# Conv feed-forward: the order of ScalarE's chunk split and first tap, and the place of a pair's activation split

## The reference, cut to what matters

```python
def causal_dwconv(u, w, b):
    C = u.shape[-1]
    y = lax.conv_general_dilated(u, w[:, None, :].astype(u.dtype), window_strides=(1,),
                                 padding=[(CONV_W - 1, 0)],
                                 dimension_numbers=('NWC', 'WIO', 'NWC'),
                                 feature_group_count=C)
    return y + b
...
def first_block(x, attn_norm, w_in, nsa_q_norm, nsa_k_norm, cmp_pos_k, cmp_pos_v, cmp_w1_k, cmp_w2_k,
              cmp_w1_v, cmp_w2_v, gla_w_gate2, gla_b_gate, gla_out_norm, w_out, ffn_norm, w_up,
              conv_w, conv_b, w_down):
...
        h = h + jnp.concatenate([o_nsa, o_gla], axis=-1) @ w_out[l]
        u = causal_dwconv(rms_norm(h, ffn_norm[l]) @ w_up[l], conv_w[l], conv_b[l])
        gate, up = jnp.split(u, 2, axis=-1)
        h = h + (jax.nn.silu(gate) * up) @ w_down[l]
    return h
...
def swiglu(hn, w_ffn_in, w_ffn_out):
    gate, up = jnp.split(hn @ w_ffn_in, 2, axis=-1)
    return (jax.nn.silu(gate) * up) @ w_ffn_out
```

## Time and profile before

| | us |
|---|---|
| median of 3 runs | 2320.32 |
| lowest, highest | 2319.63, 2327.05 |
| span of the profiled execution | 2316.6 |
| TensorE matmuls busy | 2205.7 |
| TensorE weight loads busy | 1700.6 |
| VectorE busy | 1116.4 |
| ScalarE busy | 806.4 |
| GpSimd busy | 67.8 |

### The profile page before, as it was taken

One profiled execution on the slowest core, in us unless ns is written; L12 is line 12 of the kernel. 1 busy time (PEld: TensorE's weight loads), 2 busy tenths in 40 slices (PEclk: granted clock), 3 DMA queues, 4 the chain that ended last, 5 costly groups with the idle time before them and its releaser, 6 DMA issues. The chain is left out here.

```text
span 2316.6 us, 32721 instructions
## 1 busy us (share of the span) xinstructions
PE 2205.7 (95%) x13572; PEld 1700.6 (73%) x13572; DVE 1116.4 (48%) x1800; ACT 806.4 (35%) x1310; POOL 67.8 (3%) x88
## 2 busy tenths in 40 slices
PE   8999799999999999989998999998999999999999
PEld 7776457777778898976765788766566578888887
DVE  3464675666653367654334534436332244444422
ACT  3332554333332443332224222225346533223221
POOL 0000001000000000000000000000012102000000
PEclk8999899999999999999999999999999999999999
DMA  4224001222232244331224321214721232322322
GB/s 161 65 72 154 1 1 64 82 91 82 87 105 92 78 145 130 124 110 59 66 69 146 130 92 62 70 55 150 247 69 55 91 115 91 95 96 91 98 94 91
DMA packets 78595, 218.65 MB, mean 94 GB/s; under 512 B 8688, under 2 KB 13168, under 8 KB 78448
## 3 DMA queue, kind: packets, MB, share of 16 engines
q1 hardware_dynamic: 78448, 216.57, 28.2%
HBM read 185.74 MB, written 29.75 MB: 93 GB/s over the span
## 5 line engine op out<-in xcount | busy, mean ns | idle before, releaser
L296 PE MATMUL ps<-nx_hi,whi 128*128 128x264 f32 (+1 forms) x1504 | 539.1, 358 | 17.0 <-DVE nx_lo L385 9.6
L281 DVE TENSOR_TENSOR wlo<-raw,whi 128x1024 fp32r<-128x1024 f32 x282 | 346.3, 1228 | 400.4 <-ACT whi L274 400.0
L298 PE MATMUL ps<-nx_hi,wlo 128*128 128x264 f32 (+1 forms) x1504 | 512.9, 341 | 0.0
L297 PE MATMUL ps<-nx_lo,whi 128*128 128x264 f32 (+1 forms) x1504 | 512.8, 341 | 0.0
L274 ACT ACTIVATE whi<-raw 128x1024 fp32r<-128x1024 f32 x282 | 297.8, 1056 | 520.9 <-PE ps L298 416.5
L296 PEld LDWEIGHTS ps<-nx_hi,whi 128*128 128x128 f32 x1504 | 287.0, 191 | 84.6 <-issue 45.3
L298 PEld LDWEIGHTS ps<-nx_hi,wlo 128*128 128x128 f32 x1504 | 287.1, 191 | 32.6
L297 PEld LDWEIGHTS ps<-nx_lo,whi 128*128 128x128 f32 x1504 | 287.7, 191 | 30.4 <-issue 1.9
L296 PE MATMUL ps<-x_hi,whi 128*128 128x512 f32 x528 | 209.8, 397 | 14.9 <-DVE wlo L281 14.9
L298 PE MATMUL ps<-x_hi,wlo 128*128 128x512 f32 x528 | 209.8, 397 | 0.0
L297 PE MATMUL ps<-x_lo,whi 128*128 128x512 f32 x528 | 208.4, 395 | 0.0
(11 more groups left out here) (460 smaller groups left out, 2869.9 us busy)
## 6 DMA issues: line engine op xcount, KB each, us to landing
raw<-stream_dram SPq DMA_DIRECT2D x285, 512.0 KB, 3.5
qk_spill<-ring SPq DMA_DIRECT2D x16, 264.0 KB, 2.2
qk_cols<-qk_spill SPq DMA_DIRECT2D x16, 264.0 KB, 4.0
v_spill<-ring SPq DMA_DIRECT2D x16, 264.0 KB, 2.1
v_cols<-v_spill SPq DMA_DIRECT2D x16, 264.0 KB, 4.3
dz_spill<-ring SPq DMA_DIRECT2D x16, 256.0 KB, 2.1
dz<-dz_spill SPq DMA_DIRECT2D x16, 256.0 KB, 5.1
sbk_spill<-ring SPq DMA_DIRECT2D x8, 264.0 KB, 2.1
```

The source lines that it names most:

```text
L281: dve.tensor_tensor(K.wlo[:, n % HL], K.raw[:, n % RAW], K.whi[:, n % HL].bitcast(F32), ALU.subtract).then_inc(K.s_lo, 1)
L296: pe.matmul(out, whi, xhi, start=start, stop=False, skip_group_check=skip)
L297: pe.matmul(out, whi, xlo, start=False, stop=False, skip_group_check=skip)
L298: return pe.matmul(out, wlo, xhi, start=False, stop=stop, skip_group_check=skip)
```

## The change

Only the case `conv` is altered; with `conv` false the order stays what it was. On ScalarE `hi_of` of the gate's chunk is issued before the gate's first tap, and `hi_of` of the up chunk before the up half's first tap. The high part of a pair's activation is issued behind the first tap of the next pair's gate, its low part on VectorE behind the other taps of the next pair's gate. The last pair's stays at its end. No instruction is added or taken out.

```diff
--- before.py
+++ after.py
@@ -521,21 +521,26 @@
                     scaled_hi(act, K.h[:, d], gain_ffn[:, d:d + 1], x_tile(d)[0]).then_inc(z["x_hi"], 1)
                     square("squares", "summed", d, d + 1)
                 factor_root(K, act, z)
+
+                def full_hi(p):
+                    act.wait_ge(z["act_full"], p + 1)
+                    act.activation(act_tile(p)[0], up[:, p % 2], ACT.Copy).then_inc(z["act_hi"], 1)
                 for p in range(FT):
                     pb, s = p % 2, up0 + 2 * p
                     ps = [K.ps[:, (KT + 2 * p + kind) % 4, :] for kind in range(2)]
                     if p >= 2:
                         act.wait_ge(z["act_lo"], p - 1)
-                    if p == 0:
+                    if p == 0 or conv:
                         hi_of(act, s, s, 0)
                     act.wait_ge(z["scaled"], 2 * p + 1 if conv else p + 1)
                     if conv:
                         act.activation(g[:, pb], ps[0], ACT.Identity, scale=w1[:, 0, p:p + 1, 2],
                                        bias=b1[:, 0, p:p + 1]).then_inc(z["first_tap"], 1)
                         if p > 0:
-                            hi_of(act, s, s, 0)
+                            full_hi(p - 1)
                         act.wait_ge(z["convolved"], 2 * p + 1)
                         act.activation(g[:, pb], g[:, pb], ACT.Silu).then_inc(z["silu"], 1)
+                        hi_of(act, s + 1, s + 1, 0)
                         act.wait_ge(z["scaled"], 2 * p + 2)
                         act.activation(up[:, pb], ps[1], ACT.Identity, scale=w1[:, 1, p:p + 1, 2],
                                        bias=b1[:, 1, p:p + 1]).then_inc(z["first_tap"], 1)
@@ -543,9 +548,9 @@
                         act.activation(g[:, pb], ps[0], ACT.Silu).then_inc(z["silu"], 1)
                         if p > 0:
                             hi_of(act, s, s, 0)
-                    hi_of(act, s + 1, s + 1, 0)
-                    act.wait_ge(z["act_full"], p + 1)
-                    act.activation(act_tile(p)[0], up[:, pb], ACT.Copy).then_inc(z["act_hi"], 1)
+                        hi_of(act, s + 1, s + 1, 0)
+                    if not conv or p == FT - 1:
+                        full_hi(p)
                 for _, kind, i in ends:
                     if kind == 0:
                         hi_of(act, down0 + i, down0 + i, 0)
@@ -586,6 +591,11 @@
                 lo_of(dve, up0, up0, 0)
                 factor_made(K, dve, z, rs[:])
                 dve.wait_ge(z["factor_made"], 1)
+
+                def full_lo(p):
+                    dve.wait_ge(z["act_hi"], p + 1)
+                    ah, al = act_tile(p)
+                    dve.tensor_tensor(al, up[:, p % 2], ah.bitcast(F32), ALU.subtract).then_inc(z["act_lo"], 1)
                 for p in range(FT):
                     pb, s = p % 2, up0 + 2 * p
                     for kind in range(2):
@@ -602,6 +612,8 @@
                                     y[:, 1:SEQ], ps[:, 0:SEQ - 1], w1[:, kind, p:p + 1, 1], y[:, 1:SEQ], ALU.mult, ALU.add))
                                 dve.scalar_tensor_tensor(y[:, 2:SEQ], ps[:, 0:SEQ - 2], w1[:, kind, p:p + 1, 0], y[:, 2:SEQ],
                                                          ALU.mult, ALU.add).then_inc(z["convolved"], 1)
+                                if kind == 0 and p > 0:
+                                    full_lo(p - 1)
                             elif p > 0:
                                 lo_of(dve, s + kind, s + kind, 0)
                         else:
@@ -615,9 +627,8 @@
                         dve.wait_ge(z["convolved"], 2 * p + 2)
                         dve.wait_ge(z["silu"], p + 1)
                         dve.tensor_tensor(up[:, pb], up[:, pb], g[:, pb], ALU.mult).then_inc(z["act_full"], 1)
-                    dve.wait_ge(z["act_hi"], p + 1)
-                    ah, al = act_tile(p)
-                    dve.tensor_tensor(al, up[:, pb], ah.bitcast(F32), ALU.subtract).then_inc(z["act_lo"], 1)
+                    if not conv or p == FT - 1:
+                        full_lo(p)
                 for _, kind, i in ends:
                     if kind == 0:
                         lo_of(dve, down0 + i, down0 + i, 0)
```

## The result

The changed kernel takes 2303.49 us as the median of five executions (2297.21 to 2304.18), the kernel before 2321.63 beside it (2319.63 to 2327.05). The ratio on record is 0.9903, with a 95% interval of 0.9889 to 0.9918; it is not the quotient of the two medians, which is 0.9922. By either the change is about one per cent faster. The profiled execution took 2297.21 us, its span is 2295.4 (before 2316.6); in every execution on record the time lies 1.8 us above the span. Both kernels scatter by some 7 to 11 us from one execution to the next. So sizes are read from starts and spans, and verdicts from ratios.

What follows compares the result with a forecast made beforehand. A ScalarE-VectorE ping-pong of 12.32 us a pair was taken to bound the first block's feed-forward. 227.80 - 37 x 5.60 = 20.6 us less gives span 2296.0, forecast 2299.7 us, range 2295 to 2306.

Steps and rivals of the forecast that it cites:

- From span to time: Whole kernel: the page's span lies 3.7 us under the median; the same distance turns span 2296.0 into 2299.7 us.
- What bounds: First block's feed-forward: ScalarE and VectorE wait for each other in turn, 12.32 us a pair, making TensorE start late.
- The loop: VectorE's time per pair in the up-projection when it never waits for TensorE: from 12.32 down to 8.40 us.
- The residue before the up chunk's low part: VectorE's wait for the up chunk's high part: about 0.42 us of the 1.79 stays.
- Part (a) alone is enough: Gate chunk's split ahead of the gate's first tap: alone leaves VectorE's loop at 10.47 us, already under 11.20.
- What is late next: After VectorE is level, no TensorE stall left in the stretch; last activation's low part ready some 6 us after last unit.
- The unit: One weight chunk's 24 matmuls on TensorE, taken as 5.60 us; 37 units then give 20.6 us less.
- rival 2: Second block's waits of TensorE give back gain, up to 4.3 us either way, 2296 to 2304; chance 0.12.
- Bounds: ScalarE and VectorE working at once: no cost taken; at most 24% more VectorE work, a loop of 10.3 us.
- Rival 1: VectorE's loop still binds, over 11.20 us, needing 36% more work; at 45% the time is 2312; chance 0.04.
- Rival 3: Change does nothing because transfers make TensorE late: pair stays at 12.32 us, time 2320; chance 0.04.
- Rival 4: Splits waiting for late transfers hold up ScalarE's taps; decides from landing 8.8 us, at 11 gives 2344; chance 0.03.

Runs made afterwards that it cites:

- the other session: The changed kernel run again unaltered beside the follow-up kernels: 2303.0 us over six executions, ratio 0.9919 to the kernel before.
- part (c): Only the activation's split deferred behind the next gate's taps, both weight splits left behind the first taps, against the kernel before: 2307.33 us, ratio 0.9938.
- Part (a) alone: Only the gate chunk's split put ahead of the gate's first tap, on the kernel before: 2304.84 us, ratio 0.9917.
- the first two runs with late transfers: Up-projection load of chunk n also waits until unit n-2 is used: changed kernel 2329.43 us, ratio 1.0013; kernel before 2341.97, ratio 1.0070.

## Why the prediction was right

The forecast was 2299.7 us, in a range of 2295 to 2306; measured were 2303.49 and in the other session 2303.0. The mechanism and the gain of the stretch are right. The step from span to median is not, and that the median fell into the range all the same is in part luck (see *From span to time*).

- *What bounds*: right. The ping-pong set the pace, and each part that shortens it alone makes the kernel faster.
- *The loop*: forecast 8.40 us, measured 8.22, with a backlog and with the five added products taken off again. The difference is in sizes. An instruction of VectorE that waits for nothing begins before the one ahead has ended: the scaling at 407.42 is 0.69 us long, and the low part behind it begins after 0.60, at 408.02. So a wait that goes saves its length and 0.09 us more. The same makes part (c) 0.79 us, a pair of 11.53 instead of 11.68. The residue before the up chunk's low part was put at 0.42 and is 0.44, by two terms that cancel: VectorE's two instructions after the taps were put at 1.38 us and take 1.20 (410.68 to 411.88), ScalarE's at 1.80 and take 1.65 (to 412.33). VectorE is level with TensorE in the third pair; three or four were forecast.
- *Part (a) alone is enough*: right; 10.47 was forecast, and 11.17 less its wait is 10.4 to 10.5.
- *What is late next*: right. The last activation's low part was put at 6 us after the last unit, far ahead of its use; it ends at 639.21, 6.1 us after that unit's end at 633.13, and no wait of TensorE is left.
- *The unit*: 5.60 us was taken from the second block, 5.59 is what this stretch has (11.17 a pair). The forecast of 20.6 us was 0.5 low: the stretch gave 21.1. The span was forecast at 2296.0 and is 2295.4.
- *Everything behind moves up whole* (rival 2): at 761.04 it still does. At the end the spans differ by 21.2, so next to nothing was given back in the profiled executions.
- *From span to time*: this step was wrong. The 3.7 us between the page's span and the median were taken as fixed. In every execution on record the time lies 1.8 us above its span, so 1.9 of the 3.7 were scatter. The profiled execution took 2297.21 us, 2.5 under the forecast: these 1.9, and 0.6 in the span. The median is 3.8 above the forecast, since three of the five executions took 2303 to 2304 us, and so outside the 1.5 us to which I gave a chance of 0.77. No term of the sum and no part of the range stood for the scatter of 7 us from one execution to the next; the range was wide enough because of the 4.3 us of rival 2, which the profiled executions don't show. By medians of the same session the gain is 18.1 us (2321.63 - 2303.49) and 19.3 (2322.25 - 2303.0).
- *Bounds*: ScalarE and VectorE at work together cost nothing that can be read: the low part still takes 1.23 us, the scaling 0.70.
- *Rival 1* needed 36% more work on VectorE. Three added products, 2.1 us or 26% of 7.87, were free and five, 45%, were not. *Rival 3* fell with part (a): the pair went to 11.17 us with the transfers as they were. *Rival 4* stays untested. Its 8.8 us count from a load's issue to its landing, while my late transfers land, by the sum 5.6 + 3.4, some 9 us after the end of the unit from which their split could otherwise start, and 3.4 after their issue. My expectation for the first of these runs took the one for the other. They show that a late transfer reaches TensorE in the new order sooner than in the old, by a chain that the prediction hadn't worked out.

## What to carry to other kernels

When two engines wait for each other in turn, write the loop as a sum of work and waits for one of them and hold it against the pace of the engine that ought to bound; the gain here was the difference, and no more, however many waits are removed. On an engine that takes its queue in order, put first what waits only for things that are ready long before, and behind it what waits for the partner engine: one line moved in this way (the gate chunk's split ahead of the first tap) gave the whole gain, 20.5 us by spans. What is hidden then has a margin, here about 3 us of VectorE's work a pair, that can be measured by adding idle work. The margin against late transfers is another one and has to be measured by itself: here a load issued one unit later was enough to make TensorE late.

## What the runs showed of the hardware

The granted clock of TensorE doesn't answer to the same pause in the same way every time. The changed kernel has a pause of 2.7 us that ends near 863 us, where TensorE waits for VectorE. In the execution with a span of 2295.4 us the clock stayed at full speed behind it; in the one of 2303.5 us, of the same program, it fell. The pause in either, and the stretches of 5 us from 865 on, first the shorter execution:

```profile
863.04 0.71 PE L1124 MATMUL ps<-rt,const_sb 32*128 32x264 f32 x4 [2.69 <-DVE rt L1134]
...
865.00:870.00 5.00, 5.00 (x38) 3.88 (x36) 4.10 (x10) 1.04 (x2) 0.00 (x0) 1.00 0.32 101
870.00:875.00 5.00, 5.00 (x37) 3.88 (x36) 2.77 (x5) 1.69 (x2) 0.00 (x0) 1.00 0.16 61
```

```profile
864.45 0.71 PE L1124 MATMUL ps<-rt,const_sb 32*128 32x264 f32 x4 [2.70 <-DVE rt L1134]
...
865.00:870.00 5.00, 5.00 (x25) 4.00 (x24) 4.44 (x8) 2.43 (x3) 0.00 (x0) 0.62 0.07 24
870.00:875.00 5.00, 5.00 (x22) 4.09 (x21) 1.21 (x3) 0.00 (x0) 0.00 (x0) 0.50 0.40 134
```

0.50 is the lower level, 1.2 GHz instead of 2.4, and TensorE gets through 22 matmuls instead of 37 in five microseconds. The kernel before has the same pause of 2.69 us and also spreads over 10 us; in its profiled execution the clock stayed up there. The longer execution is 0.22 us behind at the idle entry after the edited stretch (761.26 against 761.04) and 1.41 at the pause. Behind the pause the same group of matmuls (L1124) comes at 878.20 instead of 872.24, so it is 5.96 us behind, and near 1032 us it is 6.2. So the fallen clock cost 4.6 of the 8.1 us between the two. That it is the cause of the whole spread is not shown: the rest came from stretches that were not taken apart. What makes the clock fall one time and not the next stays open. In the edited stretch it was 1.00 before with pauses of 0.85 us and 1.00 after without them, so none of the gain comes from the clock. Behind the wait of 6 us in the first two runs with late transfers it fell there too.
